# A two-layer decoder trunk: sums of squares between the output tiles, and four tiles at once behind a norm

## What is computed

```python
def rmsnorm(x, g):
    return x * rsqrt(mean(x * x, axis=-1, keepdims=True) + EPS) * g

for l in range(2):
    h = rmsnorm(x, norm1_g[l])
    m, *states = mixer(h, ...)       # z = h @ w_in; HGRN2 heads, RG-LRU; merged @ w_out
    x = x + m
    h = rmsnorm(x, norm2_g[l])
    if l == 0: x = x + (silu(h @ w1) * (h @ w3)) @ w2        # dense, width 2816
    else:      x = x + moe_ffn(h, ...)                        # 8 experts, top 2, width 3584
y = rmsnorm(x, final_norm_g)
```

## Time and profile before

| what | value |
|---|---|
| device time, three runs | 1711.06, 1712.69, 1712.82 us |
| median | 1712.69 us |
| span of the profiled execution | 1714.0 us |
| PE busy | 1604.6 us (94%), 8844 matmul passes |
| DVE busy | 1358.8 us (79%) |
| ACT busy | 1011.9 us (59%) |
| POOL busy | 160.5 us (9%) |
| read from memory | 426.57 MB, 252 GB/s over the span |

### The profile page before, as it was taken

How to read it: one execution, slowest core, us unless ns; L and a number is a source line. 1 busy time by engine, 2 the same in 40 slices (tenths; PEclk the granted TensorE clock), 3 DMA queues, 4 the chain that set the end, 5 groups by cost and what they waited for, 6 DMA issues and landing times.

```text
span 1714.0 us, 24614 instructions
## 1 busy us (share of the span) xinstructions
PE 1604.6 (94%) x8844; PEld 1376.9 (80%) x8844; DVE 1358.8 (79%) x1264; ACT 1011.9 (59%) x840; POOL 160.5 (9%) x130
## 2 busy tenths in 40 slices
PE   6895889999996798999999999999999999999997
PEld 5895789998896687887888888888888788788885
DVE  5997665666697748888888888888888888888985
ACT  4644343334545326767766776776676777677672
POOL 2245400000144510000000000000000000000000
PEclk8996899999997679999999999999999999999999
DMA  8451245545343017998998998998998998998990
GB/s 260 130 160 61 92 151 182 171 164 179 124 142 105 25 57 266 368 355 291 375 359 275 370 370 281 373 355 293 362 364 288 357 368 295 360 361 299 352 341 26
DMA packets 212918, 433.00 MB, mean 253 GB/s; under 512 B 7064, under 2 KB 62800, under 8 KB 212880
## 3 DMA queue, kind: packets, MB, share of 16 engines
q1 hardware_dynamic: 208176, 421.59, 69.9%
q0 software_dynamic: 1792, 5.42, 1.0%
q10 hardware_dynamic: 2912, 5.47, 0.9%
HBM read 426.57 MB, written 5.95 MB: 252 GB/s over the span
## 4 chain that ended last, share of the span: by engine, by line
PE 76%; DVE 14%; ACT 5%; issue 3%; DMA 1%; PEld 0%; POOL 0%; DVEq 0%; ACTq 0%; SPq 0%; PEldq 0%
PE ps L1338 22%; PE ps L1340 22%; PE ps L1339 22%; DVE w_lo L773 3%; PE ps L1607 3%; ACT w_hi L482 2%; PE ps L1654 1%; PE ps L1354 1%; DVE xc L927 1%; DVE lev L899 1%; DVE sc L915 1%; DMA out_dram<-hstate 1%; DVE lev L901 1%; DVE xc L1034 1%; DVE y_f L1245 1%
## 5 line engine op out<-in xcount | busy, mean ns | idle before, releaser
L773 DVE TENSOR_TENSOR w_lo<-raw,w_hi 128x2048 fp32r<-128x2048 f32 x401 | 921.7, 2311 | 188.7 <-ACT w_hi L482 181.7
L482 ACT ACTIVATE w_hi<-raw 128x2048 fp32r<-128x2048 f32 x401 | 763.5, 1917 | 332.9 <-PE ps L1340 208.7
L1338 PE MATMUL ps<-w_hi,xg 128*128 128x512 f32 x896 | 359.4, 401 | 7.4 <-DVE w_lo L773 7.4
L1340 PE MATMUL ps<-w_hi,xg 128*128 128x512 f32 x896 | 354.5, 396 | 0.0
L1339 PE MATMUL ps<-w_lo,xg 128*128 128x512 f32 x896 | 354.1, 395 | 0.0
L1338 PE MATMUL ps<-h_hi,w_hi 128*128 128x264 f32 x736 | 216.5, 294 | 23.5 <-DVE h_lo L800 15.5
L1339 PE MATMUL ps<-h_lo,w_hi 128*128 128x264 f32 x736 | 211.5, 287 | 0.0
L1340 PE MATMUL ps<-h_hi,w_lo 128*128 128x264 f32 x736 | 211.5, 287 | 0.0
L1338 PEld LDWEIGHTS ps<-w_hi,xg 128*128 128x128 f32 x896 | 169.0, 189 | 52.5 <-DVE w_lo L773 16.7
L1340 PEld LDWEIGHTS ps<-w_hi,xg 128*128 128x128 f32 x896 | 168.8, 188 | 40.1
L1339 PEld LDWEIGHTS ps<-w_lo,xg 128*128 128x128 f32 x896 | 169.2, 189 | 36.1
(11 more groups left out here) (282 smaller groups left out, 1831.1 us busy)
## 6 DMA issues: line engine op xcount, KB each, us to landing
raw<-in_moe_w_dram SPq DMA_DIRECT2D x336, 1024.0 KB, 6.2
raw<-in_ffn_w_dram SPq DMA_DIRECT2D x33, 1024.0 KB, 5.5
raw<-in_w_in_dram SPq DMA_DIRECT2D x24, 1024.0 KB, 5.5
raw<-in_w_out_dram SPq DMA_DIRECT2D x8, 1024.0 KB, 4.9
out_dram<-hstate POOLq DMA_DIRECT2D x2, 2048.0 KB, 10.5
x_rows<-in_x_prompt_dram SPq DMA_DIRECT2D x1, 1024.0 KB
out_dram<-y_rows ACTq DMA_DIRECT2D x2, 512.0 KB
out_dram<-s_fin POOLq DMA_DIRECT2D x2, 256.0 KB, 9.8
```

Of the source, the lines that this page charges most:

```text
L482: act.activation(w_hi[:, s, :], raw[:, r, :], ACT.Copy).then_inc(hi_made, 1)
L773: dve.tensor_tensor(w_lo[:, s, :], raw[:, r, :], w_hi[:, s, :].bitcast(F32), ALU.subtract).then_inc(split, 1)
L1338: pe.matmul(out, l_hi, r_hi, start=start, stop=False)
L1340: return pe.matmul(out, l_lo, r_hi, start=False, stop=stop)
```

## The change

What it does, in five parts:

1. On ACT `norm` is taken apart into `squares`, `have_table` and `root`. Behind mixer 0 the squares of chunks 0 to 2 stand between the w_hi of units 16 and 17, the others behind it; behind mixer 1 they follow the w_hi of the last output unit, and stand inside `mixer`.
2. On PE the sums of squares of norms 1 and 3 stand between the last output tiles: chunk 0 behind tile 4, chunk 1 behind tile 5 (both ahead of a v_diag matmul), 2 and 3 behind tile 6, 4 and 5 behind tile 7, then 6 and 7. Those of norm 2 stand between the tiles of the last down projection, one each behind tiles 3 to 7, then three.
3. DVE's adds of the last down projection are split 2 and 6 around the w_lo of the second input unit, not 4 and 4.
4. On PE a new function, `project_four`, computes the first two units behind norms 1 and 2 together: for each chunk of h the three passes for each of four tiles, in banks 0 to 3. It waits at the start for both units to be split. In the feed-forward both units count as used at the end.
5. On ACT the first two z tiles of layer 1 are copied out ahead of the w_hi of its fourth unit.

```diff
--- before.py
+++ after.py
@@ -498,14 +498,14 @@
                               ).then_inc(vec_landed, 16)
             act.sem_inc(z_free, 4)
 
-            def norm(n, chunk_sum, unit=None):
-
-                have_table(ACT.Sqrt)
-                for c in range(DC):
+            def squares(chunk_sum, chunks=range(DC)):
+
+                for c in chunks:
                     act.wait_ge(x_sum, chunk_sum(c))
                     act.activation(sq[:, c, :], xT[:, c, :], ACT.Square).then_inc(sq_ready, 1)
-                if unit is not None:
-                    hi(unit)
+
+            def root(n):
+
                 act.wait_ge(ssq_done, n + 1)
                 act.activation(rstd[:, 0, :], ps[:, NORM_BANK[n], 0:T], ACT.Sqrt, bias=eps,
                                scale=1.0 / D).then_inc(root_done, 1)
@@ -536,6 +536,9 @@
             def mixer(l):
                 ib, ob = IN_BASE[l], OUT_BASE[l]
                 for u in range(IN_UNITS + SPLIT):
+                    if l == 1 and u == SPLIT:
+                        z_out(l, 0)
+                        z_out(l, 1)
                     if u >= EARLY[l]:
                         hi(ib + u)
                     if l == 0 and u == SPLIT - 1:
@@ -550,7 +553,7 @@
                         act.dma_start(hstate[:, :, :],
                                       state_hgrn[l].rearrange("b h k v -> k (b h) v")
                                       ).then_inc(st_landed, 16)
-                    if u >= SPLIT:
+                    if u > SPLIT or (l == 0 and u == SPLIT):
                         z_out(l, 2 * (u - SPLIT))
                         z_out(l, 2 * (u - SPLIT) + 1)
                     zs = lambda n: act.wait_ge(z_free, 4 + 24 * l + n)
@@ -643,14 +646,23 @@
                 hi(ob + 3)
                 if l == 0:
                     hi(FF_BASE)
+                    squares(lambda c: 8 + c + 1, range(0, 3))
                     hi(FF_BASE + 1)
+                    have_table(ACT.Sqrt)
+                    squares(lambda c: 8 + c + 1, range(3, DC))
+                else:
+                    have_table(ACT.Sqrt)
+                    squares(lambda c: 16 + 8 * FF_STEPS + c + 1)
 
 
             act.wait_ge(consts, 1)
-            norm(0, lambda c: c + 1, unit=0)
+            have_table(ACT.Sqrt)
+            squares(lambda c: c + 1)
+            hi(0)
+            root(0)
             norm_hi(0)
             mixer(0)
-            norm(1, lambda c: 8 + c + 1)
+            root(1)
             norm_hi(1)
 
 
@@ -680,10 +692,12 @@
             ff_high(FF_STEPS - 1, 0)
             hi(IN_BASE[1])
             hi(IN_BASE[1] + 1)
-            norm(2, lambda c: 16 + 8 * (FF_STEPS - 1) + c + 1)
+            have_table(ACT.Sqrt)
+            squares(lambda c: 16 + 8 * (FF_STEPS - 1) + c + 1)
+            root(2)
             norm_hi(2)
             mixer(1)
-            norm(3, lambda c: 16 + 8 * FF_STEPS + c + 1)
+            root(3)
             for n in range(6):
                 t, half = n // 2, n % 2
                 rows = TOKEN_TILES[t][2]
@@ -748,7 +762,9 @@
                     hi(EX_BASE + EX_UNITS - 1, s0)
                     gather_high(it + 1)
                     turned_high(s0 + (EX_STEPS - 1))
-            norm(4, lambda c: 16 + 8 * FF_STEPS + 8 + c + 1)
+            have_table(ACT.Sqrt)
+            squares(lambda c: 16 + 8 * FF_STEPS + 8 + c + 1)
+            root(4)
             for t, t0, n in TOKEN_TILES:
                 act.wait_ge(yt_ready, 2 * t + 2)
                 dst = (y_prompt[0, t0:t0 + n, :] if t < 2 else
@@ -1135,9 +1151,9 @@
             ff_gate(FF_STEPS - 1, 0, FF_BASE + 3 * FF_STEPS - 2)
             ff_add((FF_STEPS - 2) * DC)
             lo(IN_BASE[1])
-            ff_add((FF_STEPS - 1) * DC, range(0, 4))
+            ff_add((FF_STEPS - 1) * DC, range(0, 2))
             lo(IN_BASE[1] + 1)
-            ff_add((FF_STEPS - 1) * DC, range(4, DC))
+            ff_add((FF_STEPS - 1) * DC, range(2, DC))
             norm(2, V_N1 + 8)
             mixer(1)
             norm(3, V_N2 + 8, split_it=False)
@@ -1348,12 +1364,32 @@
                     ins = pe.transpose(ps[:, c % 4, t0:t0 + n],
                                        x_rows[0:n, t, c * P:(c + 1) * P], ident[0:n, 0:n])
                 ins.then_inc(x_turned, 1)
+            def sum_square(n, c):
+
+                pe.wait_ge(sq_ready, DC * n + c + 1)
+                ins = pe.matmul(ps[:, NORM_BANK[n], 0:T], ones[:, :], sq[:, c, :], start=(c == 0),
+                                stop=(c == DC - 1))
+                if c == DC - 1:
+                    ins.then_inc(ssq_done, 1)
+
             def norm(n):
                 for c in range(DC):
-                    pe.wait_ge(sq_ready, DC * n + c + 1)
-                    ins = pe.matmul(ps[:, NORM_BANK[n], 0:T], ones[:, :], sq[:, c, :], start=(c == 0),
-                                    stop=(c == DC - 1))
-                ins.then_inc(ssq_done, 1)
+                    sum_square(n, c)
+
+            def project_four(base, norm_n, counted):
+
+                for c in range(DC):
+                    pe.wait_ge(h_split, DC * norm_n + c + 1)
+                    for tile in range(4):
+                        _, s, _, _ = unit_of(base + tile // 2)
+                        wh = w_hi[:, s, :].rearrange("p (c n) -> p c n", c=DC)
+                        wl = w_lo[:, s, :].rearrange("p (c n) -> p c n", c=DC)
+                        cols = slice(P * (tile % 2), P * (tile % 2) + P)
+                        ins = mm3(ps[:, tile, 0:T], wh[:, c, cols], wl[:, c, cols], h_hi[:, c, :],
+                                  h_lo[:, c, :], c == 0, c == DC - 1)
+                        if c == DC - 1 and counted is not None:
+                            ins.then_inc(counted, 1)
+                return ins
 
             def project(base, j, bank, x_hi=h_hi, x_lo=h_lo, order=range(DC), parts=None):
 
@@ -1392,7 +1428,15 @@
                         scores(lev[k % 3], lev[k % 3], 1)
 
 
-                for u in range(IN_UNITS):
+                if l == 1:
+                    pe.wait_ge(split, ib + 2)
+                    pe.wait_ge(z_free, 24 * l + 4)
+                    project_four(ib, norm_n, z_done)
+                    pe.wait_ge(z_done, 24 * l + 2)
+                    pe.sem_inc(used, 1)
+                    pe.wait_ge(z_done, 24 * l + 4)
+                    pe.sem_inc(used, 1)
+                for u in range(2 * l, IN_UNITS):
                     pe.wait_ge(split, ib + u + 1)
                     for j in range(2):
                         t = 2 * u + j
@@ -1505,10 +1549,14 @@
                             pe.wait_ge(x_sum, xs + c - 3)
                         project(ob + u, j, c % 4, m_hi, m_lo, MERGE_ORDER,
                                 (m_split, DC * l) if c == 0 else None).then_inc(y_done, 1)
+                        for square in ((), (), (), (), (0,), (1,), (2, 3), (4, 5))[c]:
+                            sum_square(2 * l + 1, square)
                         if STATES_FIRST + c < NSAMPLE:
                             spread_value(STATES_FIRST + c)
                     pe.wait_ge(y_done, n0 + c + 1)
                     pe.sem_inc(used, 1)
+                sum_square(2 * l + 1, DC - 2)
+                sum_square(2 * l + 1, DC - 1)
 
             norm(0)
 
@@ -1518,7 +1566,6 @@
                 ins = pe.transpose(ps[:, 5, col:col + n], vec_rows[0:n, k, :], ident[0:n, 0:n])
             ins.then_inc(vec_turned, 1)
             mixer(0, 0)
-            norm(1)
 
             def up(base, i, bank, parts=None):
                 pe.wait_ge(split, i * RAW + (base + 1))
@@ -1526,7 +1573,7 @@
                     ins = project(base, j, bank + j, parts=parts if j == 0 else None)
                 ins.then_inc(used, 1)
 
-            def down(base, i, parity, s):
+            def down(base, i, parity, s, last=False):
                 _, sl, _, _ = unit_of(base)
                 wh = w_hi[:, sl, :].rearrange("p (j n) -> p j n", j=2)
                 wl = w_lo[:, sl, :].rearrange("p (j n) -> p j n", j=2)
@@ -1540,11 +1587,16 @@
                                   wl[:, j, c * P:(c + 1) * P], ff_hi[:, parity, j, :],
                                   ff_lo[:, parity, j, :], j == 0, j == 1)
                     ins.then_inc(y_done, 1)
+                    if last and c >= 3:
+                        sum_square(2, c - 3)
                 pe.wait_ge(y_done, s * DC + 2 * DC)
                 pe.sem_inc(used, 1)
-
-            up(FF_BASE, 0, 0, parts=(h_split, DC))
-            up(FF_BASE + 1, 0, 2)
+                if last:
+                    for c in range(DC - 3, DC):
+                        sum_square(2, c)
+
+            pe.wait_ge(split, FF_BASE + 2)
+            project_four(FF_BASE, 1, None).then_inc(used, 2)
             with pe.Fori(0, (FF_STEPS - 1) // 2) as i:
                 for k in range(2):
                     s = i * 2 + (k + 1)
@@ -1554,10 +1606,8 @@
                     pe.wait_ge(ff_g_done, s)
                     up(b + 1, i, 2)
```

(4 more changed lines are left out.)

## The result

| what | before | after |
|---|---|---|
| device time, median of the runs timed together | 1712.82 us (1710.50 to 1716.55, 7 runs) | 1720.39 us (1717.91 to 1723.33, 7 runs) |
| span of the profiled execution | 1714.0 us | 1717.0 us |
| PE busy | 1604.6 us | 1601.2 us |

The ratio is 1.0032, with a 95% interval of 1.0021 to 1.0043: the change costs 5.5 us (3.6 to 7.4). The forecast was 1720.5. The two medians of seven stand further apart, 7.6 us; I go by the ratio and its interval. The profiled execution of after took 1718.71 us, the third shortest of its seven, and its span is only 3.0 us longer than before's; the stretches inside it say more than its end. Every execution whose time and span are both on record took about 1.7 us more than its span, so by this estimate the profiled execution of before took 1715.7 us, 2.9 above the median of its seven.

The account below looks back on a forecast made before the run. PE bound the kernel, with 76% of the chain. Norm 1's +0.8 - 0.3 + 5.0 + 2.3 = +7.8, with 0 at norms 2 and 3, on the 1712.7 median gave 1720.5 us, range 1715.5 to 1723.5.

Parts of the forecast that it names:

- The wait: Behind the first four feed-forward tiles, PE waits for silu, w_hi, w_lo: 5.15 us instead of 0.12, +5.0.
- The clock behind it: In the third feed-forward unit, behind PE's new idle time: clock low for 5.1 us, +2.3.
- falling 3.15 us in and low for 6.8: Clock falls 3.15 us into PE's 4.9 us idle time, stays low 6.8, so 5.1 us of the next unit.
- Rival 1: Ahead of the third feed-forward unit, the clock stays up through the new wait: +5.5, 1718.2; chance 0.15.
- The sums: Between tiles: drain saved -0.31, 0.09 per extra group; norm behind dense feed-forward +0.7, norm behind layer 1's mixer zero.
- Rival 2: At all three norms, each interleaved sum pays a full entry, 0.31: adds 2.7, giving 1723.2; chance 0.13.
- the four exits of 0.36: At the norm behind the dense feed-forward, leaving four extra groups of sums between tiles costs PE 0.36.
- Rival 3: Six sums free at the last two norms, no later store: +1.3, 1714.0, no measurable change; chance 0.06.
- The store: Behind layer 0's mixer, two sums delay the last v_diag by 1.1 us; hstate's store and h_hi slip, +0.8.
- The prediction's other case: Behind layer 0's mixer, the store lands when it did: 0, or 1.4 by the upper bound of the groups.
- Four tiles: Computed chunk by chunk, they fill PE's holes behind the norms: -0.3 behind layer 0's mixer, -0.7 behind the dense feed-forward.
- Rival 4: In the routing stage the low clock goes, up to 12.4 us saved: -4.6, 1708.1; chance 0.03.

Follow-up runs that it names:

- two other kernels with the same wait: The kernel before with only the wait put in, 1722.20 us (ratio 1.0035); the change with mixer-output sums behind tiles 6 and 7, 1719.81 us.
- the kernel with the filled wait: The changed kernel with 20 matmuls whose result nobody reads put into PE's wait; 1717.94 us, ratio 1.0020.
- the first kernel with the wait taken out: The changed kernel with the third feed-forward unit's w_hi moved ahead of the first silu on ACT; 1714.02 us, ratio 0.9996.
- the last kernel: The changed kernel with third unit's w_hi ahead of silu, no sums before the last v_diag, last four chunks tile by tile; 1712.03 us, ratio 0.9983.
- the sums behind the last state: The changed kernel with the sums at the mixers' outputs put behind tiles 6 and 7, after all v_diag; 1719.81 us, one execution.

## Why the prediction came out right

The large term and its chain were right; the size of the whole owes something to luck. The forecast was +7.8 us on the median of before, and the ratio gives +5.5, with +7.8 above its interval (3.6 to 7.4).

1. **The wait, forecast +5.0, measured +5.04.** Shown from both sides: put alone into before it gives +6.0 us in time (3.8 to 8.4) with the clock's part in it; taken out of after in either of two ways it leaves no loss. Chain, order and releaser were as written down.
2. **The clock behind it, forecast +2.3, measured +1.65 in after's profile, +2.47 and +2.65 in two other kernels with the same wait, and -1.55 when PE was kept busy.** The step "falling 3.15 us in and low for 6.8" held for the two other kernels: both low stretches lasted 6.8 us and began inside the wait. In after's profile it failed: the fall came at the start of the next unit and the stretch lasted 3.4. So it has no single size, and the two stretches that I had measured showed me only the longer: 6.8 us behind a norm is not fixed either, behind norm 1 it was 3.4 in five of the nine kernels profiled.
3. **Rival 1, the clock stays up: refuted** for after, by its windows. What it would have brought is what the kernel with the filled wait shows.
4. **The sums.** The trace had no 4-byte matmul between tiles, and I took 0.09 for an exit and nothing for the entry. Measured: 0.12 from the last pass to the sum, as to any pass; then 0.25 to v_diag, and from v_diag to the next tile 0.66 instead of the 0.47 of before (200.48 to 200.95), so 0.44 us for one sum between tiles, with whatever it costs to enter and leave it, against 0.475 in the tail. Rival 2, an entry of 0.31 each, is refuted: that gap was the wait for PE's own last tile. So norm 3 gave -0.50 where I had written 0: the drain saved (-0.31), four sums at 0.44 instead of 0.475 (-0.14), and no exits; norm 2 gave +0.28 instead of +0.7. PE's wait for the first square was the 0.6 forecast: its sum starts 0.72 us behind the last pass (425.79 to 426.51) instead of 0.12. It was the four exits of 0.36 that weren't there: tiles 5 to 7 with a sum ahead of each take 1.17 us, of which their six passes are 0.73.
5. **Rival 3, sums that really leave the path: refuted.** The tail shrank by 1.86 us and the tiles stretched by 4 x 0.44, nearly as much, and the sums moved alone measured +0.3 us (-1.2 to +1.9).
6. **The store, forecast +0.8, measured +0.40.** Two sums slipped v_diag by 0.66, not 1.1, and the store itself came out 0.28 shorter (11.38 beside 11.66). Whether the 0.40 is the change's is open: with the sums in their old place the store landed between 20.23 and 20.95 us behind the fifth tile. The prediction's other case, a store that lands when it did all the same, is not refuted.
7. **Four tiles, forecast -0.3 and -0.7, measured -0.14 and -0.76.** The bound was the low clock behind the norm, not the chunks: right. With the clock low for 3.4 us the same four tiles took 12.91 in the first kernel with the wait taken out.
8. **Rival 4, the routing's clock.** It did come back for 3.4 us in after's profile, worth 1.6 us of time, not 12.4. But it does so with the wait alone and does not with the whole change and its sums placed otherwise, so it belongs to the execution and not to the change.

In after's profile the terms for the store, the clock, norm 2's and norm 3's sums are all smaller than forecast, by 2.0 us together. That the median still came out at 1720.39 beside 1720.5 owes something to the base. By the ratio of 1.0032, 1720.39 goes with a before of 1714.9, as the 23 and 27 runs of the experiments have it (1714.7 and 1715.0), while I started from 1712.7: 2 us too low a base under a change forecast 2 us too large. And after's profile caught the short kind of low stretch; its other runs may hold the longer.

Open is what decides between 3.4 and 6.8 us, and why the interval of the ratio stays below the distance of the two medians. Open are also the share of the store and what the last kernel gains by. None of this touches the cause of the loss, the wait.

## What to carry to other kernels

When tiles are made to end together, look at every queue that was ordered by the first of them: an entry behind a wait on it is now late, and what stands behind that entry, here a weight split that needed nothing, is late with it. Move the split ahead of the wait, and let the interleaving stop early so that the first pair still ends first. Work moved from a norm's tail to between the tiles gains only if PE had holes there; read the distance between passes first.

## What the hardware did that I had not expected

- A plain fp32 matmul of 128x264 put between split passes costs 0.44 us in all, no more than the 0.475 of one in a row, so no price for the switch shows; the 0.31 us ahead of a group of them is the wait for PE's own previous tile.
- Behind the same wait in the same place the clock was low for 3.4 us in after, and for 6.8 with the wait alone and with the sums behind the last state. Behind norm 1 it was 6.8 in four of the nine kernels profiled and 3.4 in the other five, behind norm 2 the same counts. Matmuls without a use in the wait kept it at 1.00 throughout, worth 1.55 us.
- The store of hstate, 2 MB beside the loads of weights, took 11.35 to 12.29 us in the nine profiles; where PE's list was the same up to its start (8.64 us behind the fifth tile), 11.57 to 12.29.
- The same instructions in the routing took 32.8 to 34.9 us, by when the clock came back, and before's own runs spread from 1710.4 to 1719.0 us. A difference of 2 us between two profiles of this kernel says nothing by itself.
